# One of the three weight streams of a mixture-of-experts stage moved to the GpSimd queue

## The chip, the cores and the metric

The kernel runs on one core of a Trainium2 chip. The metric is the device time of one execution in microseconds (us), as the median of several runs. A difference of under 0.2% (about 4 us here) can't be told from no change.

## The reference

One encoder layer over 256 tokens of width 2048. A mixer block and a cross attention come first; both matter here only as the work that stands ahead. Then comes the mixture of experts, which the change concerns. Cut to what is computed (the reference sorts tokens into padded blocks of 128; the sum is the same):

```python
D_MODEL, SEQ, MOE_EXPERTS, MOE_TOPK, MOE_FF = 2048, 256, 32, 2, 512
...
def hierarchical_moe(hn, w_rg, w_re, w1, w3, w2):
    p_group = jax.nn.softmax((xf @ w_rg).astype(F32), axis=-1)
    g_idx = jnp.argmax(p_group, axis=-1)
    ...
    top_v, top_i = lax.top_k(fine, MOE_TOPK)
    gate = g_gate * jax.nn.softmax(top_v, axis=-1)
    ...
    def expert_block(args):
        xblk, e = args
        return (jax.nn.silu(xblk @ w1[e]) * (xblk @ w3[e])) @ w2[e]
```

w1 and w3 (the two up matrices) are 2048 x 512 for each expert, w2 (the down matrix) is 512 x 2048, all float32. Each is 4.19 MB, so 32 experts are 402.7 MB. All of it is read once.

## The kernel before

It is one program with a hand-written instruction stream for each engine: `sp` (SyncE, which only issues transfers), `pool` (GpSimd), `pe` (TensorE), `act` (ScalarE) and `dve` (VectorE). Semaphores alone order them.

**The dense stages** (mixer and cross attention, the first 974 us) read weights in chunks of 1 MB through a ring of four buffers. SP asks for chunk c once TensorE has used chunk c-4 (`load_dense`, line 359). GpSimd works in this part only: 16 multiplications and 32 small loads of attention biases (line 456), the last at 617 us. Its program ends there.

**Routing** (974 to 1055 us) picks the experts, gathers the tokens into slots sorted by expert (`xsT`), and writes a table with the first slot of each expert. VectorE signals the table by `tab_dve`; TensorE then builds rows of slots and gates (`slot_rows`, lines 830 and 833; `row_pe`).

**The expert stage.** The expert's weights go through one ring of 12 MB, just one expert: two buffers of 2 MB for each matrix, the pairs a and b. So w1a and w1b, w3a and w3b, w2a and w2b are six transfers of 2 MB (128 partitions x 16 KB each), each with a buffer and a semaphore of its own. A pair is two of the four chunks that a matrix is used in. TensorE's `block_n(n, back)` goes through them in this order: up chunk 0 of w1 of expert n, the sums of expert n-1 (line 857), up chunk 1 of w1, the four down chunks of expert n-1 (line 871), up chunks 2 and 3 of w1, then the four chunks of w3 (line 846), each followed by a quarter of the combination of expert n-1 (line 888). So the pairs are needed in the order w1a(n), w2a(n-1), w2b(n-1), w1b(n), w3a(n), w3b(n), and so on, and are given back in that order.

Who asks for them:

- SP asks for w1 and w3 (`load_up`, line 378), after a wait for TensorE's use of the same pair of the expert before (`up_used0` for w1, `up_used1` for w3).
- ScalarE asks for w2 (`down_hi`, line 1238), after its wait on `dn_used`.

At the start SP asks for all pairs of expert 0 at about 958 us (w2 at 974). Before its loop over experts 1 to 31 stands one more request, for the final gain (line 408, 1 MB), whose destination overlaps tiles of the routing, so SP waits there for `row_pe` and for the third `tab_dve`:

```python
sp.wait_ge(S["row_pe"], 1)
sp.wait_ge(S["tab_dve"], 3)
sp.dma_start(fgain, ...).then_inc(S["fgain_in"], 16)
with sp.Fori(1, NE) as e:
    load_expert(e, e)
```

The loop over overflow blocks behind it runs only for experts with over 64 tokens.

Of the kernel before, what the change touches and what calls it, by code (L numbers as in the profile page):

```python
# [35 lines left out]
NE = 32  # L36
NG = 4
PG = NE // NG
ECH = 4
# [3 lines left out]
OVB = 2 * T // EB  # L43
# [7 lines left out]
XA_H = 4  # L51
# [76 lines left out]
def flat(v):  # L128
    if len(v.shape) == 3:
        return v.rearrange("p a b -> p (a b)")  # L130
    return v.rearrange("p a b c -> p (a b c)")
# [12 lines left out]
def program(nc, ins, out, dbg=None):  # L144
    dbg = dbg or {}
    with ExitStack() as ctx:
        def sb(name, shape, dt=F32):
            return ctx.enter_context(nc.sbuf_tensor(name, shape, dt))

        def sem(name):  # L150
            return ctx.enter_context(nc.semaphore(name))
# [10 lines left out]
        table = sb("table", [1, 128], I32)  # L162
# [115 lines left out]
        pair_up = [[arena(ring_kib[ECH * m + i], 2 * ECH, FF) for i in (0, 2)] for m in range(2)]  # L278
# [13 lines left out]
        S = {}  # L292
# [16 lines left out]
        s_up = [[sem(f"ring_up{m}_{i}") for i in range(2)] for m in range(2)]  # L309
# [19 lines left out]
        def of_expert(w, e):  # L329

            return w[e] if isinstance(e, int) else w[bass.ds(e, 1)].rearrange("a k n -> (a k) n")

        def up_chunk(e, m, i):

            return of_expert((g1, g3)[m], e).rearrange("(p k) n -> p k n", k=KT)[:, ECH * i:ECH * (i + 2), :]
# [9 lines left out]
        def _(sp):  # L345
# [28 lines left out]
            def load_up(e, n, m, i):  # L374

                if not (isinstance(n, int) and n == 0):
                    sp.wait_ge(S["up_used0" if m == 0 else "up_used1"], n * ECH + (i + 2 - ECH))
                sp.dma_start(pair_up[m][i // 2], up_chunk(e, m, i)).then_inc(s_up[m][i // 2], 16)
# [3 lines left out]
                sp.dma_start(pair_dn[i // 2], down_chunk(e, i)).then_inc(s_dn[i // 2], 16)  # L382

            def load_expert(e, n):
                for m in range(2):
                    for i in range(0, ECH, 2):
                        load_up(e, n, m, i)

            load_dense(G_WO)
            sp.wait_ge(S["chunk_used"], G_WO * NCH)  # L390
# [6 lines left out]
                sp.dma_start(wr[:, :, NG:], ins["moe_router_expert"][0].rearrange("(c p) n -> p c n", p=P)).then_inc(S["wr_in"], 16)  # L397
            sp.dma_start(routec, ins["c_route"]).then_inc(S["route_in"], 16)

            for m in range(2):  # L400
                for i in range(0, ECH, 2):
                    load_up(0, 0, m, i)
            sp.wait_ge(S["chunk_used"], (G_XO + 4) * NCH)
            for i in range(0, ECH, 2):
                load_down(0, i)
# [3 lines left out]
            with sp.Fori(1, NE) as e:  # L409
                load_expert(e, e)  # L410

            nov = sp.value_load(table[0:1, 96:97], min_val=0, max_val=OVB)
            with sp.Fori(0, OVB) as b:
                with sp.If(b < nov):
                    e = sp.value_load(table[0:1, bass.ds(b + 32, 1)], min_val=0, max_val=NE - 1)
                    load_expert(e, b + NE)
# [9 lines left out]
        @block.gpsimd  # L426
        def _(pool):
            nc.gpsimd.memset(gone, 1.0).then_inc(S["pool_step"], 1)
            nc.gpsimd.memset(buf["mv"][:, :, :, P:P + 1], 1.0).then_inc(S["pool_step"], 1)
            for s in range(2 * HG_LEVELS):  # L430
                w, half = s // HG_LEVELS, 1 << (s % HG_LEVELS)
                u = 0 if w == 0 else 1
                cut = lambda x: flat(x).rearrange("p (b u t) -> p b u t", u=2, t=half)[:, :, u, :]
                pool.wait_ge(S["h_exp"], s + 1)
                if s >= 1:
                    pool.wait_ge(S["h_pe"], s)
                nc.gpsimd.tensor_tensor(cut(hqk[s % 2]), cut(he[s % 2]), cut(buf["hff" if w == 0 else "hfb"]),
                                        ALU.mult).then_inc(S["h_mulk"], 1)


            rpb = ins["na_rpb"]
            for m in range(NA_H // 2 * NT):
                i, j = m // NT, m % NT
                if m == 0:
                    pool.wait_ge(S["h_pe"], 2 * HG_LEVELS + 1)
                    pool.wait_ge(S["h_mulk"], 2 * HG_LEVELS)
                    pool.wait_ge(S["h_mulq"], 2 * HG_LEVELS)
                if m >= 2:
                    pool.wait_ge(S["na_s"], m - 1)
                for g in range(2):  # L450
                    r = 2 * j + 1 - g
                    for u in range(2):
                        hd = 2 * i + u
                        src = bass.AP(tensor=rpb.tensor, offset=rpb.offset + hd * RPB_R * RPB_C + (7 - r) * RPB_C - 48,
                                      ap=[[1, GRID_W], [RPB_C, 4], [1, GRID_W]])
                        pool.dma_start(nbias[m % 2][g * 64:(g + 1) * 64, u, :].rearrange("p (a w) -> p a w", w=GRID_W),
                                       src).then_inc(S["bias_in0" if m % 2 == 0 else "bias_in1"], 16)

# [2 lines left out]
        def _(pe):  # L463
# [131 lines left out]
            for g, (name, fm, _, _) in enumerate(W_IN):  # L595
                if 1 <= g < G_IN - 1:
                    dense_split(g, fm, split[G_IN])
                if g == 3:

                    pe.wait_ge(S["wg_lo"], 1)  # L600
                    x_hi, x_lo = split[G_IN]
                    for k in range(KT):
                        mm(ps[0:16, 4, 0:T], wg_hi[:, k, :], x_hi[:, k, :], start=(k == 0), stop=False)
                        mm(ps[0:16, 4, 0:T], wg_hi[:, k, :], x_lo[:, k, :], start=False, stop=False)
                        last = mm(ps[0:16, 4, 0:T], wg_lo[:, k, :], x_hi[:, k, :], start=False, stop=(k == KT - 1))
                    last.then_inc(S["gate_pe"], 1)
                if g == 4:

                    pe.wait_ge(S["gate_dve"], 1)
                    for kind in range(4):  # L610
                        last = mm(ps[0:NH, 5 + kind // 2, (kind % 2) * T:(kind % 2 + 1) * T],
                                  ident[0:16, kind * NH:(kind + 1) * NH], g16, start=True, stop=True)
                    last.then_inc(S["gate_pe"], 1)

                if g == G_ML - 1:
                    ml_gates()
                if G_ML <= g < G_ML + NH:
                    ml_values(g - G_ML)
                if G_ML - 1 <= g < G_ML - 1 + NH:
                    ml_scores(g - G_ML + 1)  # L620
# [313 lines left out]
        def _(act):  # L934
# [60 lines left out]
            def w_in_out(g, name, fm, _, scale):  # L995

                if name == "mv":
                    dst = buf[name][:, 0, :, 0:P]
                elif fm:
                    dst = flat(buf[name][:, 0:2, :])  # L1000
                else:
                    dst = buf[name][:, 0, :]
                dense_out(g, dst, scale)
                if g == 0:
                    act.wait_ge(S["wg_in"], 16)
                    fn(wg_hi[:], wg, ACT.Copy).then_inc(S["wg_hi"], 1)
                if g == 2:
                    act.wait_ge(S["conv_dve"], 1)
                    fn(flat(buf["q"]), flat(buf["q"]), ACT.Silu).then_inc(S["silu_act"], 1)
                    act.wait_ge(S["conv_dve"], 2)  # L1010
                    fn(flat(buf["k"]), flat(buf["k"]), ACT.Silu).then_inc(S["silu_act"], 1)
                if g in (3, 4, 8):
                    b_ = buf[name]
                    act.wait_ge(S["proj_a"], g + 1)
                    act.wait_ge(S["proj_b"], g + 1)
                    fn(flat(b_), flat(b_), ACT.Sigmoid if g == 3 else ACT.Silu).then_inc(S["silu_act"], 1)
                if g == 5:

                    act.wait_ge(S["gate_dve"], 2)
                    step(fn(gl, gt[:, 1::2, :], ACT.Abs))  # L1020
                    step(fn(gl, gl, ACT.Exp, scale=-1.0))
                    fn(gl, gl, ACT.Ln, bias=1.0).then_inc(S["gate_act"], 1)
                    act.wait_ge(S["gate_dve"], 3)
                    fn(gr[:, 2:4, :], gr[:, 2:4, :], ACT.Exp, scale=-1.0).then_inc(S["gate_act"], 1)
# [259 lines left out]
        def _(dve):  # L1284
# [74 lines left out]
            def group_norm(m):  # L1359
# [8 lines left out]
                last.then_inc(S["y_done"], 1)  # L1368

            def w_in_out(g, name, fm, _, scale):  # L1370

                if name == "mv":
# [590 lines left out]
```

## Time and profile before

| | |
|---|---|
| runs | 2013.08, 2014.64, 2017.55 us; median 2014.64 |
| profiled execution | 2014.21 us; its span in the trace 2012.3 us |
| granted TensorE clock, mean | 0.956 |
| TensorE matmuls busy | 1893.8 us (94%) |
| VectorE, ScalarE, GpSimd busy | 831.5, 510.1, 50.4 us |
| transfers, all | 556.6 MB, mean 277 GB/s |
| queue of SP (q1) | 423.5 MB |
| queue of ScalarE (q10) | 130.0 MB |
| queue of GpSimd (q0, "software") | 2.1 MB |

The profile comes from one execution on the core. The span is what the trace covers; 1.9 us of the execution lie around it. A line of rates cuts a stretch into 40 equal slices. The share of the DMA engines is the mean over the 16 that the core has, and a row can show slightly over 1.00. An engine's busy time says little about whether it sets the end: the chain of waits, followed back from the last instruction, says that.

### The profile page before, as it was taken

What the parts mean: (1) busy time and instruction counts of PE and PEld (TensorE: products, weight loads), DVE (VectorE), ACT (ScalarE), POOL (GpSimd) and SP (SyncE); (2) the same over time, 40 slices, a digit from 0 to 9 for tenths busy, and PEclk for the clock granted to TensorE, in tenths of its full rate; (3) what the DMA queues carried; (4) which work ended last, traced back from release to release, by engine and by line L of the source; (5) the groups of instructions that cost most, each with busy time, mean ns of one, the idle gap of its engine ahead of it and who ended that gap; (6) DMA issues with size and microseconds to landing.
All of it is one profiled execution on the core that took longest, in us unless ns stands there. A gap on an engine that the chain in (4) does not pass through costs nothing.

```text
span 2012.3 us, 24848 instructions
## 1 busy us (share of the span) xinstructions
PE 1893.8 (94%) x10000; PEld 1233.4 (61%) x10000; DVE 831.5 (41%) x1196; ACT 510.1 (25%) x727; POOL 50.4 (3%) x54
## 2 busy tenths in 40 slices
PE   6999999989899999999698999999999999999995
PEld 6888799889777779978643334434434433433342
DVE  4644454788644554335432232322322222232223
ACT  4444343644333444333210100000000000001001
POOL 0000000022210000000000000000000000000000
PEclk9999899989999999999798999999999999999997
DMA  7554445334565454425609999999999999999992
GB/s 269 166 169 155 131 162 185 120 115 144 123 145 160 161 188 153 162 81 190 265 3 425 428 428 428 429 428 429 428 429 429 428 428 429 429 428 428 429 429 107
DMA packets 106973, 556.63 MB, mean 277 GB/s; under 512 B 12336, under 2 KB 12568, under 8 KB 81176
## 3 DMA queue, kind: packets, MB, share of 16 engines
q1 hardware_dynamic: 96952, 423.51, 54.5%
q10 hardware_dynamic: 8928, 130.03, 15.2%
q0 software_dynamic: 1024, 2.10, 1.5%
q8 instruction: 52, 0.85, 0.2%
q14 instruction: 17, 0.14, 0.0%
HBM read 553.51 MB, written 2.10 MB: 276 GB/s over the span
## 4 chain that ended last, share of the span: by engine, by line
PE 82%; DMA 10%; DVE 5%; ACT 2%; issue 1%; POOL 0%; DVEq 0%; SPq 0%; ACTq 0%
PE ps L846 20%; DMA arena<-in_moe_w_dram 9%; PE ps L871 8%; PE ps L534 6%; PE ps L857 6%; PE ps L535 6%; PE ps L536 6%; PE ps L528 6%; PE ps L529 6%; PE ps L530 6%; PE ps L888 3%; PE ps L818 1%; PE ps L677 1%; PE ps L496 1%; DVE w_lo L1344 1%
## 5 line engine op out<-in xcount | busy, mean ns | idle before, releaser
L846 PE MATMUL ps<-arena 128*64 128x512 f32 x2048 | 505.7, 628 | 23.7 <-DMA arena<-in_moe_w_dram 23.2
L1344 DVE TENSOR_TENSOR w_lo<-arena,w_hi 128x1024 fp32r<-128x1024 f32 x264 | 319.3, 1253 | 291.4 <-ACT w_hi L989 290.9
L989 ACT ACTIVATE w_hi<-arena 128x1024 fp32r<-128x1024 f32 x264 | 264.4, 1052 | 331.6 <-PE ps L530 176.6
L846 PEld LDWEIGHTS ps<-arena 128*64 128x64 f32 x2048 | 137.3, 141 | 286.8 <-issue 266.6
L1895 DVE TENSOR_TENSOR arena<-ps,arena 128x1024 f32<-128x1024 f32 x128 | 156.5, 1225 | 222.4 <-PE ps L888 222.4
L871 PE MATMUL ps<-arena 128*64 128x512 f32 x1024 | 230.3, 603 | 0.6 <-DVE arena L1874 0.6
L871 PEld LDWEIGHTS ps<-arena 128*64 128x64 f32 x1024 | 75.7, 142 | 157.0 <-issue 156.3
L528 PE MATMUL ps<-x_hi,w_hi 128*128 128x256 f32 x512 | 147.1, 287 | 6.9 <-DVE w_lo L1344 6.9
L1889 DVE TENSOR_TENSOR d_lo<-ps,d_hi 128x512 fp32r<-128x512 f32 x64 | 41.2, 686 | 264.1 <-ACT d_hi L1242 264.1
L530 PE MATMUL ps<-x_hi,w_lo 128*128 128x256 f32 x512 | 146.3, 286 | 0.0
L529 PE MATMUL ps<-x_lo,w_hi 128*128 128x256 f32 x512 | 146.2, 286 | 0.0
L857 PEld LDWEIGHTS ps<-stack,arena 128*128 128x128 f32 x512 | 121.9, 328 | 28.8 <-issue 28.8
L1242 ACT ACTIVATE d_hi<-ps 128x512 fp32r<-128x512 f32 x64 | 34.7, 594 | 365.8 <-PE ps L871 365.8
L857 PE MATMUL ps<-stack,arena 128*128 128x64 f32 x512 | 126.7, 402 | 0.0
L1226 ACT ACTIVATE arena<-ps 128x512 f32<-128x512 f32 x64 | 38.3, 598 | 342.4 <-PE ps L846 342.4
L528 PEld LDWEIGHTS ps<-x_hi,w_hi 128*128 128x128 f32 x512 | 99.7, 195 | 8.3 <-issue 4.5
L529 PEld LDWEIGHTS ps<-x_lo,w_hi 128*128 128x128 f32 x512 | 99.7, 195 | 0.0
L530 PEld LDWEIGHTS ps<-x_hi,w_lo 128*128 128x128 f32 x512 | 99.7, 195 | 0.0
L888 PEld LDWEIGHTS ps<-d_hi,pick 64*128 64x128 f32 x256 | 23.9, 183 | 105.2 <-DVE arena L1895 75.4
L528 PE MATMUL ps<-q_hi,w_hi 128*128 128x256 f32 x256 | 73.7, 288 | 3.5 <-DVE w_lo L1344 3.5
L1869 DVE TENSOR_TENSOR arena<-arena 128x256 f32<-128x256 f32 x32 | 13.6, 426 | 147.9 <-ACT arena L1232 147.9
L528 PE MATMUL ps<-m_hi,w_hi 128*128 128x256 f32 x256 | 74.2, 290 | 0.0
(347 smaller groups left out, 2660.6 us busy)
## 6 DMA issues: line engine op xcount, KB each, us to landing
arena<-in_moe_w_dram SPq DMA_DIRECT2D x130, 2048.0 KB, 17.7
arena<-in_moe_w_dram ACTq DMA_DIRECT2D x62, 2048.0 KB, 14.2
arena<-in_w_in_dram SPq DMA_DIRECT2D x52, 1024.0 KB, 5.1
arena<-in_xa_wk_dram SPq DMA_DIRECT2D x16, 1024.0 KB, 5.1
arena<-in_xa_wv_dram SPq DMA_DIRECT2D x16, 1024.0 KB, 5.1
arena<-in_w_out_dram SPq DMA_DIRECT2D x16, 1024.0 KB, 5.1
arena<-in_xa_wq_dram SPq DMA_DIRECT2D x16, 1024.0 KB, 5.1
arena<-in_xa_wo_dram SPq DMA_DIRECT2D x16, 1024.0 KB, 5.1
```

The lines of the kernel that those rows point to most:

```text
L528: mm(o_, hi[:, cut], a_hi[:, k, :], start=(k == 0 and n % 2 == 0), stop=False, skip_group_check=True)
L529: mm(o_, hi[:, cut], a_lo[:, k, :], start=False, stop=False, skip_group_check=True)
L530: last = mm(o_, lo[:, cut], a_hi[:, k, :], start=False, stop=(k == KT - 1), skip_group_check=True)
L534: mm(o_, a_hi[:, k, rows_], hi, start=(k == 0), stop=False)
L535: mm(o_, a_hi[:, k, rows_], lo, start=False, stop=False)
L536: last = mm(o_, a_lo[:, k, rows_], hi, start=False, stop=(k == KT - 1))
L846: last = mm(ps[rows_, m, :], xe[par][:, ECH * i + c, :], ring_up[m][i][:, c, :], start=(i == 0 and c < 2), stop=(i == ECH - 1 and c >= 2))
L857: last = mm(bank(2 + m, ECH, EB)[:, c, :], up_ev[:, m, c::ECH], stack[:], start=True, stop=True)
L871: last = mm(ps[EB * (b % 2):EB * (b % 2 + 1), 4 + b // 2, :], hT[:, i, :], ring_dn[i][:, b * 512:(b + 1) * 512], start=(i == 0), stop=(i = ...
L989: fn(hi_ring[(2 * n + u) % 4][:], ring_a[i][:, 2 * u:2 * u + 2, :], ACT.Copy).then_inc(S["w_hi"], 1)
L1344: V.tensor_tensor(w_lo[i][:, 2 * u:2 * u + 2, :], ring_a[i][:, 2 * u:2 * u + 2, :], hi_ring[(2 * n + u) % 4][:].bitcast(F32), ALU.subtract ...
L1895: V.tensor_tensor(hv, flat(ps[:, b0:b0 + 2, :]), hv, ALU.add).then_inc(S["c_add"], 1)
```

## The change

SP no longer asks for w3. GpSimd does, in a loop of its own, with the same waits on `up_used1`, and only these: it does not stand behind the request for the final gain. Its first two requests (expert 0) wait for `xs_o`, the last product of the attention in the cross-attention stage. ScalarE, VectorE and TensorE are untouched.

```diff
             def load_expert(e, n):
-                for m in range(2):
-                    for i in range(0, ECH, 2):
-                        load_up(e, n, m, i)
+                for i in range(0, ECH, 2):
+                    load_up(e, n, 0, i)
...
-            for m in range(2):
-                for i in range(0, ECH, 2):
-                    load_up(0, 0, m, i)
+            for i in range(0, ECH, 2):
+                load_up(0, 0, 0, i)
...
+            def load_second(e, n):
+
+                for i in range(0, ECH, 2):
+                    if not (isinstance(n, int) and n == 0):
+                        pool.wait_ge(S["up_used1"], n * ECH + (i + 2 - ECH))
+                    pool.dma_start(pair_up[1][i // 2], up_chunk(e, 1, i)).then_inc(s_up[1][i // 2], 16)
+
+            pool.wait_ge(S["xs_o"], XA_H)
+            load_second(0, 0)
+            with pool.Fori(1, NE) as e:
+                load_second(e, e)
+            pool.wait_ge(S["tab_dve"], 3)
+            nov = pool.value_load(table[0:1, 96:97], min_val=0, max_val=OVB)
+            with pool.Fori(0, OVB) as b:
+                with pool.If(b < nov):
+                    e = pool.value_load(table[0:1, bass.ds(b + 32, 1)], min_val=0, max_val=NE - 1)
+                    load_second(e, b + NE)
```

On SP, the place is the start of the expert stage: the four requests for expert 0, and the loop over the others (line numbers of the changed program are lower by one or two).

```order
-L378 DMA arena<-in_moe_w_dram 128x4096 x4
+L378 DMA arena<-in_moe_w_dram 128x4096 x2
 L382 DMA arena<-in_moe_w_dram 128x4096 [waits chunk_used]
 L382 DMA arena<-in_moe_w_dram 128x4096
...
 L378 ISA [waits up_used0]
 L378 DMA arena<-in_moe_w_dram 128x4096
 L378 ISA [waits up_used0]
 L378 DMA arena<-in_moe_w_dram 128x4096
-L378 DMA arena<-in_moe_w_dram 128x4096 [waits up_used1] x2
```

Two of the four requests at the start and, in the loop, the two that wait for `up_used1` have gone.

On GpSimd, the place is the end of its program, behind the last of the bias loads.

```order
+L462 DMA arena<-in_moe_w_dram 128x4096 [waits xs_o]
+L462 DMA arena<-in_moe_w_dram 128x4096
+L466 UNCONDITIONAL_BRANCH
+L466 ISA
+L462 ISA [waits up_used1]
+L462 DMA arena<-in_moe_w_dram 128x4096
+L462 ISA [waits up_used1]
+L462 DMA arena<-in_moe_w_dram 128x4096
```

The two requests for expert 0 stand behind `xs_o`, and the loop's two behind `up_used1`; between them there is no wait for the table or the slot rows.

## Rows read from the trace of the kernel before

**Rows 1.** The page: rate of all transfers in 40 slices of the span.
```profile
GB/s 269 166 169 155 131 162 185 120 115 144 123 145 160 161 188 153 162 81 190 265 3 425 428 428 428 429 428 429 428 429 429 428 428 429 429 428 428 429 429 107
```

**Rows 2.** Transfers from 1100 to 1900 us: queues, then issues with us to landing.
```profile
q1 hardware_dynamic: 15747, 229.43, 67.4%
q10 hardware_dynamic: 7777, 113.25, 33.3%
...
arena<-in_moe_w_dram SPq DMA_DIRECT2D x109, 2048.0 KB, 17.9
arena<-in_moe_w_dram ACTq DMA_DIRECT2D x55, 2048.0 KB, 14.4
```

**Rows 3.** Chain of waits, two expert blocks apart: start us, us, what.
```profile
1097.34 3.88 PE ps L857 x16
...
1125.22 3.88 PE ps L857 x16
```

**Rows 4.** Chain of waits at 1188 us, then TensorE's waits on line 846, 1060 to 1950.
```profile
1188.62 21.82 DMA arena<-in_moe_w_dram
...
1210.49 3.07 PE ps L846 x8
...
  DMA arena<-in_moe_w_dram: 40.6, 16
```

**Rows 5.** Chain of waits around the start of the expert stage.
```profile
1038.37 13.95 PE ps L846 x64
...
1055.85 8.61 DMA arena<-in_moe_w_dram
...
1064.59 3.50 PE ps L846 x8
...
1072.02 3.17 PE ps L846 x8
1075.19 6.87 PE ps L871 x32
```

**Rows 6.** Waits of SP's queue: waited for, us in total, times, longest.
```profile
SPq L408 <- PE ps L833: 16.5, 1, 16.5
```

**Rows 7.** Stretches: engines' busy us, then clock, DMA share, GB/s.
```profile
1050.00:1055.00 5.00, 5.00 (x24) 2.14 (x20) 0.00 (x0) 0.60 (x1) 0.00 (x0) 1.00 0.00 0
1055.00:1060.00 5.00, 0.13 (x1) 0.00 (x0) 0.00 (x0) 2.37 (x3) 0.00 (x0) 0.76 0.82 331
...
1075.00:1080.00 5.00, 5.00 (x26) 1.68 (x24) 0.00 (x0) 0.00 (x0) 0.00 (x0) 1.00 1.00 413
...
1965.00:1970.00 5.00, 5.00 (x26) 1.56 (x24) 2.39 (x3) 0.00 (x0) 0.00 (x0) 1.00 0.92 390
```

**Rows 8.** The page's DMA issues, SP and GpSimd: KB each, us to landing; GpSimd's issue, ns.
```profile
arena<-in_norm_final_dram SPq DMA_DIRECT2D x1, 1024.0 KB, 4.2
...
arena<-in_na_rpb_dram POOLq DMA_DIRECT2D x32, 64.0 KB, 4.4
...
L456 POOL DMA_DIRECT2D arena<-in_na_rpb_dram x32: 615/615/778, 529.6 to 617.0; - x32
```

**Rows 9.** Queues from 1140 to 1156 us: packets, MB, share of 16 engines.
```profile
q10 hardware_dynamic: 240, 3.67, 53.9%
q1 hardware_dynamic: 214, 3.18, 46.7%
```

**Rows 10.** The page's DMA queues: GpSimd's; then SP's from 934 to 948 us.
```profile
q0 software_dynamic: 1024, 2.10, 1.5%
...
q1 hardware_dynamic: 1112, 2.21, 49.8%
```

**Rows 11.** End of the attention products (timeline), and the transfers after it (stretch).
```profile
872.59 7.07 PE L771 MATMUL ps<-arena 128*128 128x256 f32 x32
...
885.00:890.00 5.00, 5.00 (x20) 4.04 (x19) 1.51 (x2) 0.00 (x0) 0.00 (x0) 0.81 0.00 0
```

**Rows 12.** VectorE's copy of the tokens, one each expert (line 1865).
```profile
L1865 DVE COPY arena<-arena x31: 694/695/696, 1041.2 to 1921.5; 128x1024 f32 x31
```

## The prediction

> **What bounds the kernel now.** I read the rates over the whole span first. From the 22nd slice to the 39th they stand at 425 to 429 GB/s, in no earlier slice above 269 [rows 1]: the expert stage is one long stream of weights at a fixed rate. The queues agree: SP's and ScalarE's shares add up to 100.7%, and each moves its bytes at the same speed (229.43 MB in 67.4% of 800 us, 113.25 MB in 33.3%, both 425 GB/s) [rows 2]. So no DMA engine is free that a third queue could put to work.
>
> Second, what TensorE would need. Two blocks stand 27.88 us apart where nothing is late [rows 3]. An expert's 12.58 MB take 12.58/0.4285 = 29.4 us. TensorE is 1.5 us faster per expert and must stand still sometimes: 16 waits, 40.6 us in all [rows 4]. The chain shows which: w1a is asked for at 1188.62 and lands 21.82 us later [rows 4], because w3a and w3b of the expert before stand ahead of it in SP's queue. Such a wait ends when the stream has come far enough, not when a request is issued.
>
> Third, the two ends of the stream. It starts at 1055.85, when SP has waited for the slot rows [rows 5, 6]; the five us before move nothing [rows 7]. It ends just before 1970, with TensorE at work [rows 7].
>
> **The change, part by part.** The end moves only if the stream ends at another time, or if TensorE's last wait falls elsewhere.
>
> *Requests saved.* Each SP request waits for TensorE's use in the order in which TensorE uses the pairs, so SP never holds one back for another. 64 issues leave SP (2 for each expert) and appear on GpSimd, at about 0.62 us each [rows 8] against 0.33; neither queue has other work then. Nothing is queued behind GpSimd's waits. Worth 0: they are covered by landing times of 14 to 18 us [rows 2]. The price of a later landing on GpSimd is bounded by its 64 KB loads (4.4 us, little of it transfer) and SP's 1 MB load (4.2 us, of which 1.05/0.4285 = 2.45 transfer, so 1.75 fixed) [rows 8]. I take 2 us from request to first bytes. In mid-stream it costs nothing, since other requests fill the engines.
>
> *Expert 0's w3* is asked for when the attention products end, at 879.7 instead of 959, and takes 4.19/0.4285 = 9.8 us. The chunks of the next stage are there already; no transfer runs from 885 to 890 [rows 11]. Worth 0, and expert 0 is needed only at 1038 [rows 5].
>
> *The start of the stream (T1).* Here something real changes. GpSimd doesn't wait for the slot rows. w3a of expert 0 is given back after 6 of its 8 up chunks, at 1038.37 + 13.95 x 6/8 = 1048.8, w3b at 1052.3 [rows 5]. So w3(1) starts at about 1050.8 where SP's first bytes come at 1056.1: **5.3 us earlier.** But the ring bounds what can be asked for before TensorE moves on: 4 pairs and the gain, 9.44 MB or 22.0 us. Before, that lasts until 1078.1, and the next request (w1a(2), released at 1075.19, bytes from about 1076.4) comes in time; the rate has no hole there [rows 5, 7]. After, it lasts until 1050.8 + 22.0 = 1072.8. And w1a(1), which TensorE waits for at 1055, now shares the engines: the two queues before take turns, 3.67 MB and 3.18 MB in 16 us [rows 9]. At 1056.1 some 5.3 x 0.4285 = 2.27 of w3's 4.19 MB are done; the other 1.92 MB go before w1a(1) is complete, 1.92/0.4285 = 4.5 us. TensorE starts expert 1 at 1069.1 rather than 1064.6, releases w1a(2) at 1079.7, and its bytes come at 1080.9. **The stream stands still from 1072.8 to 1080.9,** and then goes on as it did from 1078.1. T1 = 1080.9 - 1078.1 = +2.8 us. Bounds: if w1a(1) weren't delayed at all, the bytes would come at 1076.4, -1.7; if GpSimd's first bytes came at the 4.4 us of its small loads, w3 would have 2.95 MB left, the delay would be 6.9 and T1 +5.2. I take +2.8, since the turns are shown.
>
> *The order within the stream (T2).* w1a is no longer behind w3, w3 no longer ahead of everything: three queues take turns. The bytes are the same, so the waits sum to the same 1.5 us per expert, but they move from w1a to a pair that TensorE needs later in its block (w2b or w3b). The last wait then falls up to one expert nearer to the end: 0 to 1.5 us. A wait is also followed by slower matmuls: 8 of line 846 take 3.07 us in the chain after the wait [rows 4] against 1.87 elsewhere (6.87 for 32 of line 871 at full clock [rows 5], 1.72 for 8). That is another 0 to 1.5 near the end. I take +1.5 of 0 to 3. The last bytes aren't it: TensorE has work until well after 1970 [rows 7].
>
> *The software queue itself (T3).* The trace shows it only with loads made of 256-byte runs, 2.10 MB in 1.5% of the span (70 GB/s of engine time) [rows 10], not with 16 KB runs. The nearest rows are ScalarE's loads of this very shape, at 425 GB/s [rows 2]; further off are SP's dense loads in 2 KB runs, 2.21 MB in 49.8% of 14 us, 317 GB/s [rows 10]. GpSimd would move 31 x 4.19 = 130 MB: 306 us at 425, 410 at 317. Ends 0 and +104; I take 0, the row of the same shape.
>
> A rule that speaks against the change: VectorE's copy of 128x1024 elements takes 0.695 us once per expert [rows 12]. It stands behind the sums, early in a block; GpSimd's requests are released by the second and fourth chunk of w3, late in it. The Trainium skill (SBUF — State Buffer, on the two separate sides) says that such a copy locks GpSimd out of writing descriptors. By that rule each request that met a copy would be late by at most that time, and in a stream with 18 us of backlog the sum stays as it is.
>
> Sum: 2.8 + 1.5 + 0 = **+4.3 us**: 2014.21 + 4.3 = 2018.5 for the profiled execution (2012.3 of span and 1.9 around it). The median of the runs is 0.43 higher, so the forecast for a median is **2018.9 us**, 0.21% slower, right at the 0.2% (4.0 us) that a measurement of this kernel can tell from none.
>
> **The rivals.**
> 1. *The early start pays.* If w1a(1) isn't delayed and the stream has no hole, it ends 5.3 us earlier: 2009.3. For: nothing else is on the engines from 1050.8. Against: the ring holds one expert. It decides by whether w1a(2) can be asked for before 1072.8; before it was at 1075.2.
> 2. *Nothing changes:* T1 and T2 cancel, 2014.6. For: bytes and rate are the same. The Trainium skill (DMA: Bandwidth & Descriptors, on issuing engines) says that requests from several engines run on the same 16 DMA engines and only save issue time; by that rule alone this would be the forecast.
> 3. *The software queue moves its bytes more slowly.* In small pieces even busy slices of SP's loads run at about 410 GB/s rather than 428. On 130 MB: 317 - 304 = +13, so 2032.
> 4. *The third queue starves.* If turns go by pieces, and GpSimd's are smaller (its loads show 2.10 MB in 1024 packets, 2 KB on average [rows 10]; ScalarE's 113.25 MB in 7777, 14.6 KB [rows 2]), then w3 gets perhaps an eighth beside one other queue. w1 and w2 (8.4 MB, 19.6 us) go first, w3 the 8.3 us left of each 27.9, though it needs 9.8. The shortfall gathers into gaps of the stream while TensorE waits, and with turns lost in each block I estimate a wait of 9 us at every third expert: 10 x 9 less the 46 us (31 x 1.5) that TensorE waits anyway, +44, so 2058. The Trainium skill (DMA: Bandwidth & Descriptors, on SWDGE and HWDGE) gives a packet of up to 4096 B as preferred and the packet as the unit of turns, which would favour this rival.
>
> **Chances.** Forecast case 0.55 (2012 to 2023, by the bounds of T1 and T2), rival 1 0.15, rival 2 0.10, rival 3 0.14, rival 4 0.06. Faster by over 0.2% (under 2010.6): rival 1 and a little of the forecast case, 0.17. Slower (over 2018.7): half of the forecast case and rivals 3 and 4, 0.29 + 0.20 = 0.49. Within: 0.34. The range leaves out the better half of rival 1 and all of rival 4 with the worst of 3: 2009.5 to 2034.
>
> **What would show it.** Right: transfers from about 1051; TensorE starts expert 1 near 1069; a stretch near 1073 to 1081 without transfers, then 428 GB/s to the end, about 1972; w1a lands in some 15 us and waits end on w2b or w3b. Wrong: no hole (rival 1), shares that sum to 1.00 at under 425 GB/s (rival 3), w3 landing after 25 us or more with holes all along (rival 4).

## The result, and the profile after

The changed kernel takes 2019.14 us (median of 15 runs, 2015.16 to 2022.03); the kernel before, measured beside it, 2014.34 (15 runs, 2013.08 to 2017.55). The ratio is 1.0022, with a 95% interval of 1.0014 to 1.0030. That is 4.8 us by the medians, slower by a hair more than the 0.2% that can be told from nothing. The forecast was 2018.9 us, and 0.49 on slower.

The page of the changed kernel, rates over the span (against [rows 1]):

```profile
GB/s 272 166 169 150 141 155 186 126 105 147 120 146 172 153 181 168 148 167 190 178 70 367 426 430 428 428 429 428 429 428 428 429 428 429 428 427 430 428 414 99
```

The plateau is the same 428. What is new stands at its start: 70 GB/s in a slice that had 3, then 367 where there were 425. The stream starts earlier and then fails to be full. The same stretch in the chain of waits (start, us, what; against [rows 5]):

```profile
1037.32 13.96 PE ps L862 x64
...
1054.11 0.33 SPq L406
...
1054.80 13.66 DMA arena<-in_moe_w_dram
...
1068.60 3.68 PE ps L862 x8
...
1078.03 6.87 PE ps L887 x32
```

w1a of expert 1 lands 13.66 us after its request instead of 8.61. GpSimd's requests stand ahead of it (timeline of its queue):

```profile
878.91 1.12 POOL L462 DMA_DIRECT2D arena<-in_moe_w_dram  x2 [262.33 <-PE ps L787]
1048.54 0.54 POOL L462 DMA_DIRECT2D arena<-in_moe_w_dram  x1 [168.51 <-PE ps L862]
1051.92 0.54 POOL L462 DMA_DIRECT2D arena<-in_moe_w_dram  x1 [2.85 <-PE ps L862]
```

And the transfers by stretch (busy us of PE, PEld, DVE, ACT, POOL, then clock, DMA share, GB/s; against [rows 7]):

```profile
1050.00:1055.00 5.00, 4.08 (x18) 1.72 (x14) 0.00 (x0) 1.48 (x3) 0.54 (x1) 1.00 0.89 367
1055.00:1060.00 5.00, 0.00 (x0) 0.00 (x0) 0.00 (x0) 1.48 (x2) 0.00 (x0) 0.65 1.01 431
...
1070.00:1075.00 5.00, 5.00 (x18) 3.06 (x15) 0.19 (x1) 0.38 (x1) 0.00 (x0) 0.65 0.47 200
1075.00:1080.00 5.00, 5.00 (x23) 2.37 (x25) 2.10 (x5) 0.00 (x0) 0.00 (x0) 1.00 0.19 46
1080.00:1085.00 5.00, 5.00 (x26) 1.73 (x24) 0.00 (x0) 0.00 (x0) 0.00 (x0) 1.00 0.99 416
```

By the packets' own times nothing moves from 1072.9 to 1079.2. From 1100 to 1900 us three queues share what two had, at the old rate (packets, MB, share of 16 engines; against [rows 2]):

```profile
q0 software_dynamic: 7942, 115.71, 34.0%
q1 hardware_dynamic: 7816, 113.64, 33.4%
q10 hardware_dynamic: 7778, 113.27, 33.3%
```

The last wait for a transfer in the chain has moved from w1a to the end of a block, to w3b of expert 30, and TensorE's waits stand at the down products too (line 887). The rows are TensorE's waits from 1060 to 1960 us: us in total, times, longest. PE is the matmuls, PEld the weight loads that run ahead of them; both stand still in the same wait, so their times overlap and can't be added.

```profile
1916.49 26.68 DMA arena<-in_moe_w_dram
...
1943.22 3.01 PE ps L862 x8
```
```profile
PE ps L862 <- DMA arena<-in_moe_w_dram: 25.0, 7, 14.5
PEld ps L887 <- DMA arena<-in_moe_w_dram: 17.2, 10, 2.8
PEld ps L862 <- DMA arena<-in_moe_w_dram: 13.9, 8, 2.5
PE ps L887 <- DMA arena<-in_moe_w_dram: 9.3, 6, 1.9
```

**Where 4 us of span went.** Three points cut the span: SP's first request for expert 1, the last packet of the weight stream (from the packets' times), and the end.

| | before | after | difference |
|---|---|---|---|
| SP's first request for expert 1 | 1055.85 | 1054.80 | -1.05 |
| from there to the stream's last packet | 915.3 | 918.2 | +2.9 |
| from there to the end of the span | 41.1 | 43.3 | +2.2 |
| span | 2012.3 | 2016.3 | +4.0 |

The first row is scatter of the routing: SP's first request lies between 1053.1 and 1056.6 in the runs below that start in the old way.

What stands behind the stream's last packet can be split once more, at the start of expert 31's down product, the last one (rows of the chain before and after):

```profile
1976.87 9.92 PE ps L871 x32
```
```profile
1982.31 8.39 PE ps L887 x32
```

From the stream's last packet (1971.2 and 1973.0) to this product are 5.7 us before and 9.3 after, 3.6 more. The product itself is 1.5 us shorter after, with the same 32 matmuls. TensorE stands still for 0.57 us ahead of it in both runs and the granted clock falls (1.00 is 2.4 GHz, the lower level is 1.2 GHz, and figures between are means over both). Before, it is 0.57 from 1975 to 1980 and 0.74 from 1980 to 1985; after, 0.66 from 1980 to 1985 and 1.00 from 1985 to 1990. From its end on, all runs take the same 25.6 us.

### The profile page after: what moved, and what is told of

Its sections match the earlier page's. It is cut to its first block, busy times and chain, and to the rows that moved or that the text cites. A ratio compares the mean times of both kernels' runs of the same rounds, so it can differ in the third digit from the quotient of the medians.

```text
span 2016.3 us, 25043 instructions
## 1 busy us (share of the span) xinstructions
PE 1886.6 (94%) x10000; PEld 1230.9 (61%) x10000; DVE 831.4 (41%) x1196; ACT 509.9 (25%) x727; POOL 85.2 (4%) x119
## 4 chain that ended last, share of the span: by engine, by line
PE 83%; DMA 9%; DVE 5%; ACT 2%; issue 1%; POOL 0%; DVEq 0%; SPq 0%; POOLq 0%; ACTq 0%
PE ps L862 21%; PE ps L887 9%; DMA arena<-in_moe_w_dram 9%; PE ps L550 6%; PE ps L551 6%; PE ps L552 6%; PE ps L544 6%; PE ps L545 6%; PE ps L546 6%; PE ps L873 5%; PE ps L904 4%; PE ps L834 1%; PE ps L693 1%; DVE w_lo L1360 1%; PE ps L512 1%
## 5 line engine op out<-in xcount | busy, mean ns | idle before, releaser
L462 POOL DMA_DIRECT2D arena<-in_moe_w_dram x64 | 34.5, 539 | 1299.4 <-PE ps L862 1031.8
## 6 DMA issues: line engine op xcount, KB each, us to landing
arena<-in_moe_w_dram ACTq DMA_DIRECT2D x62, 2048.0 KB, 17.4
```

## Experiments

Each time stands beside the kernel before, measured in the same session on the same chip; the sessions' medians of before were 2012.64, 2013.86 and 2013.35 us. The expectations name times on the level of the first measurement (2014.3), so compare differences from before. "Remainder" is the time from the stream's last packet to the end of the span, in the profiled execution; "hole" is a stretch without any packet once the stream has begun.

### GpSimd's loop waits for the slot rows as well

```diff
             load_second(0, 0)
+            pool.wait_ge(S["row_pe"], 1)
+            pool.wait_ge(S["tab_dve"], 3)
             with pool.Fori(1, NE) as e:
```

> GpSimd's loop over experts 1 to 31 now also waits for the slot rows and the third table signal, so w3(1) is asked for together with w1(1) at 1055 us and not 5 us earlier. Theory (the ring holds one expert; what delays the stream is that w3(1) shares the engines with w1(1), and the early start pays part of that back): all of w3(1) is still to come, so w1a(1) lands after (1.05 + 2.10 + 3.15) MB, some 14.7 us after its request, the hole before w1a(2) grows, T1 rises from +2.8 to +5.7, and with the order's +1.5 to +2.2 the time is 2021 to 2023 us, 2 to 4 us slower than the changed kernel. Rival (it is the early start itself that does harm, by colliding with the last routing work): 2014 to 2017. Rival (the third queue costs all of it in mid-stream): no difference from the change, 2019.

2018.83 us against 2012.64; ratio 1.0031 (1.0020 to 1.0041), +6.2 by the medians. In the trace w1a(1) takes 13.19 us to land:

```profile
1053.08 13.19 DMA arena<-in_moe_w_dram
```

Giving the early start up doesn't help, so the early start itself isn't what harms: that rival falls. The delay of w1a(1) comes from sharing, whether w3 starts earlier or at the same time. Its landing time is less than the 14.7 forecast, since GpSimd's first bytes (1057.5) come 1.2 us behind SP's. The hole shrinks to 2.5 us, because the known work was begun later. From SP's first request to the last packet are 919.2 us, 3.8 more than before where the expectation had 5.7. How much slower it is than the changed kernel stays open: +6.2 and +4.8 are 1.4 apart, less than the 2 forecast, and the intervals overlap.

### w1a of expert 1 first

```diff
             load_second(0, 0)
+            pool.wait_ge(s_up[0][0], 32)
             with pool.Fori(1, NE) as e:
```

> GpSimd's loop waits first for the landing of w1a of expert 1, so that pair has the engines to itself as before, while SP's w1b keeps the stream full until w3 comes. Theory: T1 falls to 0 (w1a(1) lands in about 8.6 us, no stretch without transfers behind it, TensorE starts expert 1 at the old time after the routing); only the order within the stream is left, so 2015.8 to 2016.6 us, some 3 us faster than the changed kernel and 1.5 to 2.2 slower than before. Rival (all of the loss is in mid-stream or at the tail): 2019 as the change. Rival (all of it is the start): 2014.3 as before.

2014.86 us; ratio 1.0010 (1.0001 to 1.0019), +2.2. The chain and the stretches:

```profile
1055.07 8.94 DMA arena<-in_moe_w_dram
```
```profile
1070.00:1075.00 5.00, 5.00 (x19) 2.48 (x20) 2.29 (x5) 0.00 (x0) 0.00 (x0) 0.66 1.00 426
1075.00:1080.00 5.00, 5.00 (x28) 1.55 (x24) 0.00 (x0) 0.00 (x0) 0.00 (x0) 1.00 1.01 419
```

w1a(1) lands in its old time, the hole is gone, and the loss at the start with it: from SP's first request to the last packet are 915.8 us, before 915.3. By the medians one wait of GpSimd, once, halves what the change costs (+2.2 against +4.8 and +4.9); the intervals overlap a little. About 2 us are left, the size of T2.

### An early start on SP, two queues

SP asks for expert 1 ahead of the final gain, whose waits held it back; the loop then runs from expert 2.

```diff
+            load_expert(1, 1)
             sp.wait_ge(S["row_pe"], 1)
             sp.wait_ge(S["tab_dve"], 3)
             sp.dma_start(fgain, ...).then_inc(S["fgain_in"], 16)
-            with sp.Fori(1, NE) as e:
+            with sp.Fori(2, NE) as e:
```

> The kernel before, all of w1 and w3 on SP, but SP asks for expert 1 ahead of the final gain and so ahead of the wait for the slot rows; the gain comes behind it. Theory (the expert stage is one stream of fixed rate; only the time at which it starts and holes in it count): the first pair of w1 is released at about 1042 us, the stream starts near 1043 instead of 1056, and TensorE doesn't stand at 1055; 9.44 MB last until about 1065 and w1a(2) is asked for near 1063, so there is no hole. The stream ends 13 us earlier: 2001 to 2003 us. Rival (the ring holds one expert, so an early start is always given back by a hole): 2010 to 2014.

2000.88 us; ratio 0.9939 (0.9926 to 0.9953), -11.8. The rates:

```profile
1040.00:1045.00 5.00, 5.00 (x26) 1.71 (x24) 0.04 (x1) 0.60 (x1) 0.00 (x0) 1.00 0.78 282
...
1055.00:1060.00 5.00, 5.00 (x22) 4.20 (x22) 0.91 (x3) 1.08 (x2) 0.00 (x0) 0.88 1.01 433
1060.00:1065.00 5.00, 5.00 (x22) 1.52 (x20) 1.38 (x3) 0.00 (x0) 0.00 (x0) 0.78 0.96 367
```

The stream begins at 1041.2, has no hole and ends at 1957.0, 14.2 us earlier than before; the remainder is 43.0, 1.9 longer. So most of an early start is kept when it brings the transfers that TensorE needs first. The change started early too, but with the pairs that are needed last.

### The same move in the changed kernel

The diff is the same, on the changed kernel (where `load_expert` is w1 alone).

> The changed kernel with the same move: SP asks for w1 of expert 1 ahead of the gain and the slot rows. All three queues start early, w1(1) before w3(1). Theory: same stream as the early start on SP alone, but with three queues taking turns; the difference between the two is the order's cost alone, +1.5 to +2.2, so 2003 to 2005 us. Rival (the order costs nothing, all of the change's loss was the delay of w1a(1)): equal to the early start on SP within 0.7 us. Rival (GpSimd's queue costs more when it shares for long): over 4 us slower than the early start on SP.

2002.69 us; ratio 0.9948 (0.9935 to 0.9962), -10.0, and 1.8 us behind the two queues with the same start. That is near the forecast T2, but the two intervals overlap, and the two traces show no difference: both have a stream of 916.8 and 916.9 us and a remainder of 43.0. So this pair doesn't show that T2 exists with an early start.

### The changed kernel again, in the second session

> The changed kernel once more, beside the kernel before and the next three on one chip, so that the differences can be read without the step from chip to chip. All theories: +4 to +5 us over the kernel before.

2018.71 us against 2013.86; ratio 1.0023 (1.0014 to 1.0032), +4.9. The profiled execution was the slowest of the 11 (2021.94). Its hole was 8.0 us, its remainder 43.2, and from SP's first request to the stream's last packet it took 920.5 us, 5.2 more than before. TensorE's second chunk of w1 shows why the hole was longer: it took 3.61 us here and 1.87 in the first execution, so w1a(2) was released later.

### The down matrix on GpSimd, in the kernel before

ScalarE no longer asks for w2; GpSimd does, with the same waits. Experts' overflow blocks keep ScalarE's requests.

```diff
+            pool.wait_ge(S["chunk_used"], (G_XO + 4) * NCH)
+            for i in range(0, ECH, 2):
+                pool.dma_start(pair_dn[i // 2], down_chunk(0, i)).then_inc(s_dn[i // 2], 16)
+            with pool.Fori(1, NE) as e:
+                for i in range(0, ECH, 2):
+                    pool.wait_ge(S["dn_used"], e * ECH + (i + 2 - ECH))
+                    pool.dma_start(pair_dn[i // 2], down_chunk(e, i)).then_inc(s_dn[i // 2], 16)
```

> The kernel before with the down matrix asked for by GpSimd in place of ScalarE: two queues as before, in the same order, but one of them the software queue. Only T3 is tested. Theory (16 KB runs cost GpSimd's queue what they cost the others, 425 GB/s of engine time): within 0.7 us of the kernel before. Rival (a request of GpSimd costs later landings or slower bytes that count): 2 to 13 us slower than before.

2013.11 us; ratio 0.9998 (0.9989 to 1.0007). From 1100 to 1900 us:

```profile
q1 hardware_dynamic: 15755, 229.45, 67.4%
q0 software_dynamic: 7777, 113.25, 33.3%
```

The software queue moves the same bytes in the same share as ScalarE's did [rows 2]. T3 is 0 here (-0.8 us by the medians), and the rival that gave it a price falls.

### One queue, in the order of need

SP asks for all six pairs, each behind TensorE's use of its buffer, in the order in which TensorE goes through them. ScalarE's requests are gone.

```diff
-            with sp.Fori(1, NE) as e:
-                load_expert(e, e)
+            def load_down_after(e, i):
+                sp.wait_ge(S["dn_used"], e * ECH + (i + 2 - ECH))
+                load_down(e, i)
+
+            load_expert(1, 1)
+            with sp.Fori(2, NE) as e:
+                load_up(e, e, 0, 0)
+                load_down_after(e - 1, 0)
+                load_down_after(e - 1, 2)
+                load_up(e, e, 0, 2)
+                load_up(e, e, 1, 0)
+                load_up(e, e, 1, 2)
+            load_down_after(NE - 1, 0)
+            load_down_after(NE - 1, 2)
```

> All six pairs asked for by SP, in one queue and in the order in which TensorE needs them and gives them back; the start as before. Tests whether taking turns costs anything (T2). Theory: the bytes and the rate are the same, so the stream ends at the same time; waits for transfers fall on w1a as in the kernel before or are spread, and the last one lies no later: 0 to 1.5 us faster than before. Rival (the order is worth nothing in either direction, the 2 us of the three queues are something of the software queue): equal to before within 0.5 us. Rival (one queue can't keep the engines full): slower, with a rate under 425 GB/s.

2007.60 us; ratio 0.9964 (0.9950 to 0.9977), -6.3: four times what the theory allowed. From 1100 to 1900 us one queue fills all engines:

```profile
q1 hardware_dynamic: 23526, 342.73, 100.6%
...
arena<-in_moe_w_dram SPq DMA_DIRECT2D x166, 2048.0 KB, 22.2
```

The stream's last packet is where it was (1970.8 us, before 1971.2); the remainder is 35.0 us instead of 41.1. So the gain lies wholly in how far TensorE has come when the stream ends. The last wait in the chain:

```profile
1932.09 24.51 DMA arena<-in_moe_w_dram
...
1956.73 1.94 PE ps L859 x8
```

In this order nothing lands before what TensorE is waiting for. With two queues w2 has landed ahead of need in such a wait, with three w1 and w2 have, and all that has come too early is work that TensorE still has to do when the stream ends. The traces show it at the last expert. The first column is how long w3a(31) had lain in its buffer when TensorE first used it, the second the time from the stream's last packet to the last down product, the third that product (all in us):

| | w3a(31) lay | to the last down product | the product |
|---|---|---|---|
| before; down_on_pool (two queues) | 5.2; 4.9 | 5.7; 5.4 | 9.9; 9.9 |
| changed kernel; again (three) | 9.5; 8.2 | 9.3; 7.9 | 8.4; 9.7 |
| gate_loop; w1_first (three) | 8.4; 7.6 | 8.8; 8.1 | 9.7; 8.5 |
| early_sp (two); early_three (three) | 7.0; 6.8 | 7.4; 7.4 | 9.9; 9.9 |
| one_queue (one) | 0.1 | 0.5 | 8.8 |
| early_one; again (one) | 0.4; 0.4 | 0.8; 0.8 | 8.4; 10.0 |

One queue brings TensorE to the last down product 5.2 us sooner after the stream's end than two, and three bring it there 2.2 to 3.6 us later (against before), except with an early start, where two and three are alike. The third column takes 8.4 to 10.0 us with the granted clock, even in two executions of one kernel; of the 6.1 us of remainder that one_queue gains in its trace, 1.1 are that. As an estimate, 5.2 us of the stream are 5.2 x 0.4285 = 2.2 MB, about one pair that no longer lies ahead of need.

### One queue and the early start together

`load_expert(1, 1)` moves ahead of the final gain.

> One queue in the order of need, and expert 1 asked for ahead of the final gain and the slot rows. Theory: the early start's -12 us and the order's 0 to -1.5 add up: 12 to 13.5 us faster than the kernel before, the fastest of all. Rival (order worth nothing): equal to the early start with SP and ScalarE, 11.8 us faster than before.

1995.43 us; ratio 0.9905 (0.9890 to 0.9920), -18.4 us, ahead of both kernels of this case. Only the last experiment below is as fast. The two gains add up (11.8 + 6.3). Again in the third session:

> The same version with the gain inside the stream, on the same chip as the two above, to read the difference from. All theories: 18 to 19 us faster than the kernel before.

1996.68 us; ratio 0.9917 (0.9903 to 0.9930).

### w3 only behind w1: a miss

```diff
                         pool.wait_ge(S["up_used1"], n * ECH + (i + 2 - ECH))
+                        pool.wait_ge(s_up[0][1], n * 16 + 16)
```

> The changed kernel, but GpSimd asks for w3a and w3b of an expert only once w1b of that expert has landed. Three queues stay, but w1 no longer takes turns with w3: the order within the stream is that of the kernel before (w1, then w3; w2 beside both). Theory (what counts in mid-stream is how much has landed ahead of what TensorE waits for, not the number of queues): the stretch from the stream's last packet to the end of the span falls from 44.6 us back to the 42.4 of the kernel before; at the start the stream may stand still for some 2 us between w1b(1) and w3a(1), since nothing else has been asked for. So 0 to +2.5 us over the kernel before. Rival (a third queue costs by itself): the stretch stays at 44 to 45, +2 to +5.

2086.41 us; ratio 1.0374 (1.0355 to 1.0393), +73. The order is as intended, but the price was overlooked: the request for w3 now waits for a landing. The chain shows a loop (SP's w1b lands, GpSimd asks, w3b lands, TensorE goes on until it has used the next w1b, and only then can SP ask again):

```profile
1294.14 21.52 DMA arena<-in_moe_w_dram
...
1340.59 14.82 DMA arena<-in_moe_w_dram
...
1356.69 20.85 DMA arena<-in_moe_w_dram
1377.54 0.04 issue
1377.59 3.45 PE ps L863 x8
```

The loop takes two experts: from GpSimd's request for w3b at 1294.14 to the one at 1356.69 are 62.55 us, of which 21.5 and 14.8 are landings and 24.7 TensorE's work between them. GpSimd's pairs of requests come at every expert (timeline):

```profile
1324.99 1.19 POOL L463 DMA_DIRECT2D arena<-in_moe_w_dram  x2 [30.31 <-DMA arena<-in_moe_w_dram]
1356.04 1.19 POOL L463 DMA_DIRECT2D arena<-in_moe_w_dram  x2 [29.86 <-DMA arena<-in_moe_w_dram]
1387.50 1.19 POOL L463 DMA_DIRECT2D arena<-in_moe_w_dram  x2 [30.27 <-DMA arena<-in_moe_w_dram]
```

From the first pair of the loop (1069.10) to the last (2020.99) they are 31.7 us apart on average; the stream alone would need 29.4. That is some 2.4 us more for each of 31 experts, 73 us in all, the whole of the loss. (The expectation counts the remainder 1.3 us longer than this text does; the step from 42.4 to 44.6 is the same 2.2.) The run tells nothing of turns between w1 and w3 at the full rate, so that question stays with the three runs above.

### The final gain behind the stream

In the fastest version the gain's request (1 MB) goes behind all experts.

> The fastest version so far (one queue in the order of need, expert 1 asked for early), with the final gain's 1 MB asked for after all experts and so out of the stream. Theory (the ring of one expert bounds what can be asked for before TensorE moves on): without the gain 8.4 MB last from about 1043 to 1062.5, w1a(2) brings bytes at about 1064, so a hole of 1 to 2 us takes most of the 2.45 us back: 0.5 to 1.5 us faster than with the gain in the stream. Rival (bytes taken out of the stream count in full): 2.4 us faster.

1994.98 us against 1996.68 with the gain inside; ratios 0.9910 (0.9895 to 0.9925) and 0.9917 (0.9903 to 0.9930). The difference is not resolved. The hole is there, as the ring's bound says, 2.0 us by the packets' times; the rate without and with the gain in the stream:

```profile
1060.00:1065.00 5.00, 5.00 (x20) 1.50 (x18) 1.45 (x4) 0.00 (x0) 0.00 (x0) 0.73 0.53 180
```
```profile
1060.00:1065.00 5.00, 5.00 (x18) 1.55 (x16) 1.68 (x4) 0.00 (x0) 0.00 (x0) 0.68 1.05 410
```

## Why the prediction was right

**Requests saved: 0.** Right, as far as it was tested: moving 62 requests from ScalarE to GpSimd and 2 from SP (down_on_pool) changed nothing either.

**Expert 0's w3: 0.** Right: asked for at 878.9, with the engines idle, and nobody waited for it later.

**The waits before.** [rows 4] were read as 40.6 us of standing still. The view adds the matmuls (PE, 23.2 us in 8 waits) and the weight loads (PEld, 17.4 us in 8), which stand still together. TensorE's own waits are the 23.2 us, 9.5 of them the first one at 1055. Much of the rest of the 1.5 us per expert is slower work at a lower clock: after a wait of 2.69 us that ends at 1651.68, two chunks take 3.51 and 3.17 us instead of 1.87, at a granted clock of 0.64 to 0.79. The sum doesn't use the 40.6.

**T1, +2.8 us.** The measured time from SP's first request to the stream's last packet grew by 2.9. Its steps, in the order of the text:

| step | forecast | measured |
|---|---|---|
| w3's first bytes | 1050.8 | 1049.8 |
| delay of TensorE's start of expert 1, from SP's request | +4.5 | +5.1 (13.80 against 8.74) |
| stretch without transfers | 1072.8 to 1080.9 | 1072.9 to 1079.2; 8.0 us long in the second execution |
| rate before and after it | 428 | 431, then 416 to 428 |

The sum is closer than its steps: an earlier start and a longer delay cancelled, and TensorE's second chunk of w1 ran at the full clock (1.87 us where before it took 3.17), which gave back a microsecond. That chunk was luck: in the second profiled execution it took 3.61 us, and T1 came out at +5.2, the upper bound of the text. So the mechanism and the bounds are shown, not the +2.8 to a tenth. w1_first shows the cause by taking it away: with w3 kept back until w1a(1) has landed, the hole and, by the medians, half of the loss go. The gated loop shows that starting early was no harm in itself.

**T2, +1.5 of 0 to 3.** The size is near: the remainder grew by 2.2 in the profiled execution, and w1_first stands 2.2 over before (0.2 to 3.8 by its interval, so hardly resolved). The waits moved where the text put them, to w2 and w3. But the working behind the term was wrong. It took the place of the last wait as the effect. The kernel before had its last wait of over 0.7 us at 1798.5 and down_on_pool at 1884.7, and their remainders are 41.1 and 40.9; in the changed kernel it moved to 1943.2, five experts nearer to the end and not one. What counts is how much has landed ahead of need when the stream ends (the table under one_queue). By it three queues cost 3.6 us in the profiled execution, more than the bound; the last down product, faster by 1.5 at a higher clock, gave part back. So the match with +1.5 is partly luck. A bound "below 0" was never asked for, since the text took the old order as the natural one, and one queue is 6.3 us under it. For this change it made no difference; for the next idea it would have.

**T3, 0 of 0 to 104.** Right. GpSimd's packets average 14.6 KB like ScalarE's (115.71 MB in 7942; the data go in packets of 16384 B), the three queues' shares are equal, and w2 on that queue costs nothing. With that, rivals 3 and 4 are out. The Trainium skill (DMA: Bandwidth & Descriptors, on SWDGE and HWDGE) gives packets of up to 4096 B as preferred; runs of 16 KB weren't cut to that here.

**The rule on VectorE's copy.** GpSimd's 64 issues took 537 to 573 ns each:

```profile
L462 POOL DMA_DIRECT2D arena<-in_moe_w_dram x64: 537/537/573, 878.9 to 1949.9; - x64
```

In the changed kernel no request met the copy; the nearest starts are 6.0 us apart. In w3_behind_w1, where a landing sets the time of the request, 11 of 62 requests did meet one. They took 537 to 549 ns like the others, and the first bytes came 1.24 us after the first of two requests, met or not; two of the copies took 0.78 us instead of 0.69. So the rule (the Trainium skill, SBUF — State Buffer, on the two separate sides) shows no delay of an issue or of first bytes here. Whether a met request's later bytes were held up, these rows can't say: its landing was somewhat late in some cases (8.8, 10.5 and 10.6 us for w3a; without a copy 7.5 to 8.9, once 11.2), with other queues' bytes beside it.

**Rival 1** was decided where the text put it. w1a(2) was released at 1078.0, after the known work had run out. Early starts that carry w1 first do pay, 11.8 us. **Rival 2**, that moving requests between engines is neutral, by the rule on issuing engines in the Trainium skill (DMA: Bandwidth & Descriptors), holds for the rate (428 GB/s with one, two and three queues) and fails for the time: against two queues with the same start, one is 6.3 us faster and three (gate_loop) are 6.2 slower, since a queue is also an order.

## What to carry to other kernels

Where a stream of transfers already fills the engines, as here with one, two or three queues, another queue adds no rate, so look at three other things: when it starts, whether a bounded ring leaves it nothing to fetch, and how much lands ahead of need while something else is waited for. One queue in the order of use kept the third at its least here; a queue more lets late-needed data take turns with what is waited for. In a loop, order requests by position in a queue that is already full and not by a wait for a landing: that wait became part of the cycle, at 73 us. Once, ahead of the loop, such a wait paid.

## What the runs showed of the hardware that I had not expected

- One queue alone fills all 16 DMA engines with 2 MB loads in 16 KB runs: 100.6% and 428 GB/s over 800 us, the same as two or three.
- GpSimd's queue brought its first bytes 1.2 us after the issue began when the engines were idle (1048.54 to 1049.8), though its small loads had taken 4.4 us to land. In mid-stream it took 3.6 to 4.2 us.
- Order in the queue, at the same bytes, rate and end of the stream, is worth 6.3 us in 2014.
- After a wait of 2.69 us TensorE's next chunks ran at a granted clock of 0.64 to 0.79, and were 3 us slower, on top of the wait; by 1664 the clock was 1.00 again.
